# Mixing rows, up projection and down projection of a hybrid decoder block: three stages written as one

## What is computed

```
x = x + rms_norm(merged @ w_mix_out, norm_mix_post_w)
h = rms_norm(x, norm_ffn_pre_w)
up = causal_dwconv(h @ ffn_w_up, ffn_conv_w, ffn_conv_b)      # 3 taps
gate, val = _split(up, (FFN_D_FF, FFN_D_FF))                   # 2816 each
ff = (jax.nn.gelu(gate, approximate=True) * val) @ ffn_w_down
return x + rms_norm(ff, norm_ffn_post_w)
```

## Time and profile before

| | us |
|---|---|
| median of three runs | 2322.45 (2322.39 to 2326.39) |
| the profiled execution | 2322.67 |
| its span, first to last instruction | 2321.2 |
| PE busy in the span | 2171.3 (94%) |
| DVE busy | 1265.4 (55%) |
| ACT busy | 732.5 (32%) |
| mean granted TensorE clock | 0.970 |

### The profile page before, as it was taken

The page is one execution under the profiler, slowest core; times in us unless marked ns, Lnnn a source line. Parts: engine busy times, 40 slices in busy tenths (PEclk is TensorE's granted clock), DMA queues, the critical chain, the costliest instruction groups (busy, mean ns, idle before and its releaser), DMA issues. The chain is left out here.

```text
span 2321.2 us, 29172 instructions
## 1 busy us (share of the span) xinstructions
PE 2171.3 (94%) x10502; PEld 1795.7 (77%) x10502; DVE 1265.4 (55%) x1585; ACT 732.5 (32%) x1377; POOL 466.2 (20%) x486
## 2 busy tenths in 40 slices
PE   7999999989899899899699998969999999979997
PEld 7888889867677677777588886848888888868785
DVE  6845552178888889889543224534333433442522
ACT  4322220124434434444343113322222222243432
POOL 1000011165665566466200000000000000000000
PEclk9999999989999999999799999979999999989999
DMA  6222342143343343332354223211111111033353
GB/s 215 66 89 90 108 155 90 66 138 98 107 139 102 99 137 107 115 118 86 133 180 154 73 81 109 100 65 45 51 48 45 45 54 45 27 120 94 106 147 86
DMA packets 124754, 228.41 MB, mean 98 GB/s; under 512 B 24656, under 2 KB 69840, under 8 KB 124656
## 3 DMA queue, kind: packets, MB, share of 16 engines
q1 hardware_dynamic: 81408, 159.78, 22.1%
q0 software_dynamic: 13040, 46.41, 6.0%
q10 hardware_dynamic: 30208, 20.98, 2.8%
HBM read 174.42 MB, written 52.69 MB: 98 GB/s over the span
## 5 line engine op out<-in xcount | busy, mean ns | idle before, releaser
L163 PE MATMUL fu_ps<-h_hi,fu_w_hi 128*128 128x512 f32 x704 | 274.0, 389 | 10.9 <-DVE fu_w_lo L1762 10.9
L165 PE MATMUL fu_ps<-h_hi,fu_w_lo 128*128 128x512 f32 x704 | 277.8, 395 | 0.0
L164 PE MATMUL fu_ps<-h_lo,fu_w_hi 128*128 128x512 f32 x704 | 276.6, 393 | 0.0
L1768 DVE SCALAR_TENSOR_TENSOR fu_xc<-fu_ps,fu_cw,fu_xc 128x1023 f32<-128x1023 f32 x44 | 56.4, 1283 | 297.6 <-ACT fu_xc L1742 297.6
L163 PE MATMUL ps_zg<-u_hi,g_hi 128*128 128x512 f32 x448 | 186.0, 415 | 0.0
L165 PE MATMUL ps_zg<-u_hi,g_lo 128*128 128x512 f32 x448 | 177.3, 396 | 0.0
L164 PE MATMUL ps_zg<-u_lo,g_hi 128*128 128x512 f32 x448 | 176.3, 393 | 0.0
L163 PEld LDWEIGHTS fu_ps<-h_hi,fu_w_hi 128*128 128x128 f32 x704 | 132.5, 188 | 41.0 <-DVE fu_w_lo L1762 11.3
L164 PEld LDWEIGHTS fu_ps<-h_lo,fu_w_hi 128*128 128x128 f32 x704 | 132.6, 188 | 31.0
L1742 ACT ACTIVATE fu_xc<-fu_ps,fu_cw 128x1024 f32<-128x1024 f32 x44 | 53.1, 1207 | 326.7 <-PE fu_ps L165 326.7
L163 PE MATMUL fd_ps<-fd_s_hi,fd_w_hi 128*128 128x512 f32 x352 | 140.7, 400 | 15.4 <-DVE fd_w_lo L1978 15.3
(11 more groups left out here) (276 smaller groups left out, 5015.8 us busy)
## 6 DMA issues: line engine op xcount, KB each, us to landing
fu_w_raw<-in_w_up SPq DMA_DIRECT2D x44, 512.0 KB, 3.6
mx_a_row<-acs_s SPq DMA_DIRECT2D x32, 512.0 KB, 3.9
g_raw<-in_w_xbc SPq DMA_DIRECT2D x24, 512.0 KB, 3.6
tok_s<-fr_work POOLq DMA_DIRECT2D x24, 512.0 KB, 4.0
fd_w_raw<-in_w_down SPq DMA_DIRECT2D x32, 384.0 KB, 3.1
fd_w_raw<-in_w_down SPq DMA_DIRECT2D x32, 320.0 KB, 2.9
g_raw<-in_w_gate SPq DMA_DIRECT2D x16, 512.0 KB, 5.0
raw_pieces<-in_w_z SPq DMA_DIRECT2D x16, 512.0 KB, 4.7
```

What stands on the lines that cost most here:

```text
L163: pe.matmul(dst, s_hi, m_hi, start=first, stop=False)
L164: pe.matmul(dst, s_hi, m_lo, start=False, stop=False)
L165: return pe.matmul(dst, s_lo, m_hi, start=False, stop=last)
L1768: dve.scalar_tensor_tensor(xc[:, j, 1:SEQ], ps[:, j, 0:SEQ - 1], cw[:, bass.ds(i, 1), j, 1], xc[:, j, 1:SEQ], ALU.mult, ALU.add).then_inc( ...
```

## The change

`mix_rows`, `ffn_up` and `ffn_down` become one function `back` in one stage (prefix `bk_`), with tiles placed at fixed addresses that overlap where one use has ended (ff lies over the mixing weights, for example). The two stage ends between them fall away. Further:

- One ring of two slots (`w_raw`, `w_hi`, `w_lo`) carries up and down weights. The eight mixing pieces come through five buffers, the two slots of the ring and the three of `y_t`; x goes into the first two tiles of `merged`, and its first two loads are issued ahead of the pieces 5 to 7.
- The first two up weight tiles are split within the norm steps of the token tiles 3 and 4 (`split_up(0, j)`), and on PE 36 matmuls of the first token half stand between `turn(5)` and `turn(7)`, and nine more behind `turn(7)`.
- In the last up pair the first five half tiles of `ff` are split into tiles of their own (`e_hi`, `e_lo`) before that pair's products are done; the others go into the storage of `h_hi` and `h_lo` as soon as the last up product has ended. Six down blocks are split between them.
- Blocks are now of 5, 6, 6 and 5 k steps. For three pairs of output tiles, the first, the last of the first half and the first of the second half, both tiles take block b before either takes block b + 1 (`crossed`). The second half's splits follow in the crossed pair q = 3, block by block.
- The down part has no loops; the norm row `f_post` goes into `xc[:, 1]`, so its load waits until the last `ff` tile is written, and it stands in SP's queue behind the eighth down block.

```diff
-def mix_rows(nc, A, merged, x2_s, h_hi, h_lo, ident):
+def back(nc, A, merged, x2_s, out, ident):
+    BLK = ((0, 5), (5, 6), (11, 6), (17, 5))
...
+        def crossed(q):
+            return q in (0, PAIRS - 1, PAIRS)
+        def block_of(q, p):
+            return (p // 2, p % 2) if crossed(q) else (p % NBK, p // NBK)
...
         @block.sync
+            for k in range(5):
+                load_mix(k)
...
+            sp.wait_ge(s_lo_done, 2)
+            for t in range(2):
+                load_x(t)
+            for k in range(5, KT):
+                load_mix(k)
...
+            for m in range(8):
+                load_down(m)
+            sp.wait_ge(ff_done, FT)
+            sp.dma_start(f_post, A["ffn_post_row"].partition_broadcast(P)).then_inc(post_in, 16)
+            for m in range(8, 2 * PAIRS * PB):
+                load_down(m)
...
         @block.scalar
+            for q in range(2 * PAIRS):
+                for p in range(PB):
+                    m = PB * q + p
+                    if 6 <= m + 2 < 2 * PAIRS * PB:
+                        split_down(m + 2)
+                    if q == PAIRS - 1 and p % 2:
+                        act.wait_ge(block_used, m + 1)
+                        for k in range(BLK[p // 2][0], sum(BLK[p // 2])):
+                            split_ff(1, k)
+                    if q and p == 1:
+                        squares(2 * q - 2) if crossed(q - 1) else None
+                    if q and p == 3:
+                        squares(2 * q - 1)
...
         @block.tensor
+            pe.wait_ge(y_ready, 6)
+            pe.wait_ge(w_lo_done, 1)
+            pe.wait_ge(h_lo_done, TH)
+            up(0, 0, range(0, 4))
             turn(NT - 2)
+            up(0, 0, range(4, KT))
+            pe.wait_ge(y_ready, 7)
+            pe.wait_ge(w_lo_done, 2)
+            up(1, 0, range(0, 5))
             turn(NT - 1)
+            up(1, 0, range(5, KT))
+            pe.wait_ge(h_lo_done, NT)
             for j in range(2):
+                up(j, 1).then_inc(product_done, 1)
...
+            for q in range(2 * PAIRS):
+                if q == 1:
+                    pe.wait_ge(conv_done, 2 * FT)
+                if q >= 2:
+                    pe.wait_ge(f_out, 2 * q - 2)
+                for p in range(PB):
+                    m = PB * q + p
+                    b, j = block_of(q, p)
+                    pe.wait_ge(w_lo_done, 2 * FT + m + 1)
```

More of the change, by code:

```diff
@@ new lines, in _ @@
+            act.wait_ge(cw_in, 16)
+            for j in range(2):
+                act.wait_ge(stored[j], 16 * NT // 2)
+            pair(0, True)
+            with act.Fori(1, FT - 1) as i:
+                pair(i, False)
+            i = FT - 1
+            for k in range(EARLY):
+                split_ff(0, k)
+            act.wait_ge(product_done, 2 * FT - 1)
+            act.wait_ge(ff_done, i)
+            taps(i, 0)
+            split_down(0)
+            act.wait_ge(conv_done, 2 * i + 1)
@@ new lines, in _ @@
+            split_down(4)
+            for k in range(13, 17):
+                split_ff(0, k)
+            split_down(5)
+            for k in range(17, FT):
+                split_ff(0, k)
+            for q in range(2 * PAIRS):
[11 more added lines that the diff above has]
+                        squares(2 * q - 1)
+                        if q == PAIRS:
+                            root(0)
+                    if p == NBK + 2 and not crossed(q):
+                        squares(2 * q)
+                    if p + 1 == ends(q, 0):
+                        copy_out(q, 0)
+                copy_out(q, 1)
@@ L1965, in _ @@
+            squares(2 * KT - 1)
             root(1)
@@ L1968, in _ @@
         def _(dve):
[L1969 removed]
+            own, down = Chain(dve, dve_own), Chain(dve, down_own)
             def do(ins):
[L1972 to L1979 removed]
@@ new lines, in _ @@
+            for t in (NT - 2, NT - 1):
+                split_h(t)
+            dve.wait_ge(cw_in, 16)
+            with dve.Fori(0, FT - 1) as i:
+                pair(i)
+            i = FT - 1
+            for k in range(EARLY):
+                split_ff(0, k)
+            conv(i, 0)
+            split_down(0)
+            split_down(1)
+            for k in range(5, 8):
+                split_ff(0, k)
+            split_down(2)
+            for k in range(8, 11):
+                split_ff(0, k)
@@ L2076, in _ @@
-            for h in range(2):
-                pair(h, 0, True)
-                with pe.Fori(1, PAIRS) as i:
-                    pair(h, i, False)
-            turn(2 * KT - 1, 1)
+                    last = pe.transpose(ps_f[:, f % 2, t], d_f[:, f % 2, t * P:(t + 1) * P], ident[:])
+                last.then_inc(f_turned, 1)
+            for k in range(KT):
+                pe.wait_ge(s_lo_done, k + 1)
+                pe.wait_ge(m_lo_done, k + 1)
+                for t in range(2):
+                    mix(t, k)
```

721 lines of the change are left out of this document (333 added, 388 removed).

## The result

The changed kernel takes 2284.32 us (median of four runs, 2280.78 to 2286.45) where the kernel before, on the same chip, takes 2323.47. The ratio is 0.9823, with a 95% interval from 0.9807 to 0.9839. Two runs further down, one of e13 (2759.86 us) and one of the last kernel (3664.56 us), ran at a mean granted clock of 0.745 and 0.555 and are left out.

A forecast was written before the change was run, and what follows sets the result against it. PE's queue was taken as the bound, winnable only where PE waits or runs at the lower clock; -17.3 - 14.5 - 2.7 = -34.5 us against 2322.67 gave 2288.2, forecast as 2288, range 2283 to 2297 (about 0.9).

The forecast's parts named there:

- Mixing to up products: From turn(5) to the second token half: 48 up products done at 1547.1, 17.5 us earlier; with 0.2 added back, -17.3.
- 0.2 of stall behind it: Next product, a pair later: its weight split takes 5.7 us, covered by only 5.5 us of value tile matmuls; adds 0.2.
- The step of the up part: Up products: nothing to win, 0.229 us per matmul kept; any other step was listed as a sign of being wrong.
- Up to down products: Start of the down products: 15.8 us of waits and slow matmuls go, new waits of 1.0 and 0.3 come; -14.5.
- That for the norm row: Down part: DVE waits for the late f_post load ahead of block 6, giving PE 1.0 us of new wait.
- That for block 8: Down part: block 8's load, among the residual's four loads, lands late; 0.3 us put down for it.
- Boundary of the halves: Between token halves in the down part: wait of 2.27 and seven slow matmuls (1.4) go, 1.0 comes back; -2.7.
- The small waits cost the clock: Rival: each of three new waits is followed by a slow stretch of 1.4 us; +4.2, hence 2292.4; chance 0.17.
- The clock is not lost behind `turn(6)` and the down waits are hidden: Rival: turn(6) takes 0.8 us, tile 7's split ends 1.9 earlier, 2.3 of new down waits go; 2284; chance 0.07.
- The up products don't do what they are for: Rival at the turns: lower clock persists (+6.2), split tiles lengthen the norm chain; gain 8.7, hence 2297; chance 0.04.
- A long run loses the clock: Rival: from 1534.78 us on, nearly unbroken work brings the lower clock; 100 us of it gives 2335; chance 0.03.
- No difference: Rival for the whole kernel: gains and new waits cancel; chance 0.01.

The follow-up runs named there:

- e13: Changed kernel with the ring and all tiles behind it 128 bytes further on; 2299.12 us (one run).
- the last kernel: Changed kernel with split_h(t - 2) ahead of tile t's second norm, 24 up products between turn(5) and turn(6), squares ahead of six ff splits; 2272.29 us, 0.9761.
- e3: Changed kernel without up products between the turns: all 48 of the first token half come behind turn(7); 2291.22 us, ratio 0.9853.
- The six runs on addresses: Kernel before with a 64-byte pad, and five changed kernels with h, ring or tiles behind it moved by 64 or 128 bytes; up steps 0.2267 to 0.2333 us.
- e12: Changed kernel with h_hi, h_lo and the ring all 64 bytes lower; 2285.12 us, ratio 0.9817.
- e6: Changed kernel with all 24 first-half products of the gate tile between turn(5) and turn(6); 2280.10 us, ratio 0.9795.
- the padded kernel: Kernel before with 64 unused bytes behind the up stage's tap weights, moving its weight ring to distance 0 from h; 2320.22 us, ratio 0.9976.
- e8: Changed kernel with the first down pair done one output tile after the other, splits in that order, instead of crossed; 2296.57 us, ratio 0.9864.
- e2: Changed kernel with the ring and all tiles behind it 64 bytes further on; 2300.48 us, ratio 0.9891.

## What the prediction had right, and the term that failed

The time came out 7 us under the forecast and below its range. The waits were found where they were said; what failed is the step of the up products, taken over unchanged with nothing put down for it, and that is 4.3 us of the 7. A second, smaller term is the 1.3 us of new waits put against the down products, which did not come.

**Mixing to up products, forecast -17.5 and 0.2 of stall behind it, measured -17.7.** The step by step count held: `turn(6)` waits 6.6 us, is at the lower level with a few matmuls, `turn(7)` at once, and the 48th product at 117.67 us behind the first mixing product where the working gives 1547.1 - 1429.4 = 117.7. The split up tiles and the reordered loads cost nothing that can be seen. By e3, 9.8 of the 17.7 are the early products; the other 7.9 go with the stage end and the weight load behind it, which no kernel here tried alone. The stall of 0.2 at the first value tile was there too (a step of 0.43 at 1562.8 and one of 0.33 behind it, 0.3 in all).

**The step of the up part, forecast unchanged, measured shorter: this is the term that failed.** The text said of these 480 us that there was "nothing to win there", took 0.229 per matmul over into every count, and gave "a step other than 0.229 in the up part" only as a sign of error. 2063 steps became shorter by 0.0022 us. From the 48th up product to the last it takes 468.07 instead of 472.19 us, and with that stall and a longer first step inside (0.4), the matmuls themselves give back 4.5. The six runs on addresses show the cause: merging the stages placed the ring at a distance of 0 instead of 64 from h. It is no effect of the merged stage, and the kernel before gets it from a pad of 64 bytes. The diff said that tiles are now at fixed addresses, and the trace of before held the hint: at a clock of 1.00 the up products took 0.2289 a step and the mixing and down products 0.2272 and 0.2274. That the same instruction had two speeds in one trace was not asked about.

**Up to down products, forecast -14.5, measured -16.3.** From the last up to the first down product 11.44 became 0.23 us, and the down part is 7.9 shorter, of which 2.8 belong to the boundary. The gross of 15.8 was good; the waits put against it did not come. That for the norm row, put at 1.0, exists on DVE (1.08 us, in the row above) but not on PE: DVE had the last ff split when the forecast said (20.8 us behind the end of the up products against 21.4), the load took 3.7 instead of 4.5 us, and block 6 was split at 2043.06, some 0.4 before PE wanted it. That for block 8, put at 0.3, had 0 as well, but in two other kernels it is there, 1.07 us in e12 and 1.64 in e6: beside the four loads of the residual the block's own load took 4.8 us in the changed kernel, 6.4 in e12 and 7.0 in e6. So 1.3 between the bounds 0 and 4 was no bad place, and that the outcome lies at the low end is partly luck. The loads of the changed kernel, issue to landing, beside the earlier trace rows:

```profile
bk_ff<-x_s POOLq DMA_DIRECT2D x4, 512.0 KB, 5.8
bk_w_raw<-in_w_down SPq DMA_DIRECT2D x3, 320.0 KB, 2.9
bk_xc<-in_ffn_post_row SPq DMA_DIRECT2D x1, 512.0 KB, 3.7
bk_w_raw<-in_w_down SPq DMA_DIRECT2D x1, 384.0 KB, 6.8
```

**Boundary of the halves, forecast -2.7, measured -2.8.** The wait stands where it was said and costs 0.87 with the first matmul's longer start, for 1.0. Half of the gain is less sure than the sum made it, though: it counts the seven slow matmuls of the earlier trace rows as gone (1.4), and in the trace of the padded kernel, where this part is the same code, the same wait of 2.27 us has none behind it:

```profile
2179.05 0.47 PE L163 MATMUL fd_ps<-fd_s_hi,fd_w_hi 128*128 128x512 f32 x1 [2.27 <-DVE fd_w_lo L1979]
```

(The next steps are 0.31, then 0.23.) **The tail** is 16.3 instead of 16.8 us.

The sum: 17.7 + 4.1 + 16.3 + 2.8 + 0.6 = 41.5 us. The forecast misses by 4.3 in the step (its stall of 0.2 counted), 1.8 at the down products, and 0.9 in the rest. With the step alone put right it would have been 2284.

**The rivals.** *The small waits cost the clock*, 0.17: refuted. The waits of 0.31 and 0.72 us are followed by steps of 0.23, and so are 1.07 (e12), 1.64 (e6) and 1.45 (e8) in the other kernels. The rule of the Trainium skill, page "TensorE: Matmul & The Clock Gate", section "A second HAM failure mode: psum-queue depth-cycling", by which frequent short idles make the clock swing, is not borne out by any of these rows; in this kernel 2292 would have been too high by 11. *The clock is not lost behind `turn(6)` and the down waits are hidden*, 0.07: half of it came, the hidden waits; the clock was lost. *The up products don't do what they are for*, 0.04: refuted by e3. *A long run loses the clock*, 0.03: refuted. From 1543.5 to 2274 us, 730 us, the granted clock stays at 1.00. No difference, 0.01: refuted.

**The range** held the unknown waits and the clock on the slow side, and on the fast side only what the second rival gave. It had no room for a gain that was in no term.

## What to carry to other kernels

Before a stage is taken as "PE busy, clock 1.00, nothing to win", divide its length by its matmuls and compare with the kernel's other stages of the same shape: a difference of 1% is worth a run, and the start addresses of its two operands (their distance modulo 256 bytes, best 0 here) are the first thing to try. Where stages are merged, cover the seam with work of the next stage placed between the last waits of the old one, and look at which engine queue's order, not which amount of work, ends each wait that is left. Where an operand must be split on the way to PE, consider letting two output tiles share each split before counting on an earlier start, and keep the splits that PE waits for out from behind those that wait for PE.

## What the runs showed of the hardware

- The step of a 128x512 fp32r matmul at the full clock depends on where its operands start: in the up and mixing products 0.2267 to 0.2272 us at distance 0, 0.2289 at 64, 0.2324 to 0.2330 at 128 and 0.2333 at 192 bytes (moving minus stationary, modulo 256). The exception: three of eight mixing tiles of e2, at 64, stepped at 0.2333. The Trainium skill, page "TensorE: Matmul & The Clock Gate", section "Back-to-back issue gap", makes the spacing out of the columns, the weight load and the clock; here 3% hang on a fourth thing.
- A wait of 3.51 us in e8 was followed by five steps of 0.23 and then by slow ones, one of 2.62 in the padded kernel by four and then by slow ones, and one of 2.27 in the kernel before by two; but the same wait of 2.27 in the padded kernel was followed by none, and neither were those of 2.02 us and less. How long a wait is does not alone say what the clock does behind it; what else counts was not tested.
- The four loads of the residual took 5.8 us instead of the 7.2 of the earlier trace rows, and a 384 KB weight load beside them 6.8 instead of 5.0. A 320 KB weight load issued just behind them took 4.8, 6.4 and 7.0 us in three kernels that issue the same loads (changed, e12, e6), and 2.9 with nothing beside it: in company, the time to landing moved by 2 us between such traces.
